# The decode tokens' share of the conformer convolution: taps over the state rows summed once ahead of the group loop

## The chip, the cores and the metric

The kernel runs on one core of one Trainium2 chip. The metric is the device time of one execution in microseconds, as the median of several runs. The core has five engines that run side by side: TensorE (PE; its weight loads are shown as PEld), VectorE (DVE), ScalarE (ACT), GpSimd (POOL) and SyncE (SP), which issues most of the transfers.

## The reference, cut to what matters

One layer of a hybrid decoder is computed for 560 tokens: 8 running sequences with 4 new tokens each (32 "decode" columns), 16 meta tokens and 512 prompt tokens (528 "prompt" columns). One of its two branches is a depthwise causal convolution of 31 taps over 1024 channels:

```python
a = glu_v * jax.nn.sigmoid(glu_g)
a_full = jnp.concatenate([conf_buf, a], axis=1)      # conf_buf: 30 rows of state per running sequence
new_conf_buf = a_full[:, -(CONF_K - 1):]
a = causal_dwconv(a_full, conf_dw_w, conf_dw_b)      # CONF_K = 31 taps, one weight per tap and channel
```

For a decode token r (0 to 3) of a sequence, output r is the sum over the taps j = 0 to 30 of w[j] times row r + j of a_full. Rows 0 to 29 come from the state and rows 30 to 33 are the new tokens. So tap j of token r reads a new token only where r + j is 30 or more, which is in 10 of the 4 x 31 products. The prompt starts from zeros. The other branch is a state-space mixer (convolution of 4 taps, chunked scan, gated norm). After both come output products, and a mixture of 32 experts.

## The kernel before, in words

The kernel has a first stage (`trunk`), an output stage (`mixer`) and the routing and experts. The change is in `trunk` alone. It holds the channels on the 128 partitions and the tokens along the columns.

**Prologue.** State, scales and tokens are loaded, turned by TensorE into the channel layout (`fill`), and copied out of the PSUM banks pS and pT by VectorE (lines 902 to 928). The 30 state rows of the 8 sequences land in `stC`, 240 columns for each of 8 blocks of channels. Then TensorE multiplies the step sizes (line 698, into pC), VectorE waits for that (`s_dtp`), and a short chain over VectorE, ScalarE and TensorE ends in `s_pro`.

**Group loop.** It has eight trips, g = 0 to 7, each over 128 channels of the conformer branch and one of eight groups of the other. TensorE multiplies ten weight blocks a trip (`block`, line 731, each 8 x 3 weight loads with two products of 304 and 256 columns behind each). Every block needs its weights loaded (SP), rounded (ScalarE, line 504) and the rest taken (line 230: POOL for blocks 0 to 5, VectorE for blocks 6 to 9). Blocks 6 to 9 are cut in halves, and between the halves stand the six chunks of the scan: TensorE `stage1(j)` (lines 748 to 757), ScalarE `chunk(j)` (lines 588 to 597), POOL `xtl`, `hTd` and the decay rows of the next chunk (lines 444, 451, 434), VectorE `stage1(j)` (lines 1012 to 1016, which ends with tile Lx), TensorE `stage2(j)` (from line 771, which reads Lx), VectorE `stage2(j)` (to line 1042). The order is written out by hand on each engine, and each engine works in its own order and waits at semaphores.

**The 31 taps.** VectorE spreads them over the trip (`conf_tap`, `taps`): two before its `stage1(0)`, two in front of each of `stage2(0)` to `stage2(4)`, eight before `stage2(5)`, four after the new states, seven at the very end. Each tap is two instructions: a small one of 32 columns from `a_s` (30 state rows and 4 new ones for each sequence) and a big one of 528 columns from `a_p`. All go through the helper on line 871, but for tap 0 on lines 969 and 970. The big one is linked: `k.link` makes VectorE wait until it has ended, so the next tap's small one starts behind it. The small one has no wait behind it. Tap 30 writes `aout`, after a wait for the store of the last group's `aout` (`s_ast`), and SP stores it on line 310 when `s_cconv` comes.

**POOL** copies, at the start of a trip, the group's scales (line 410), the state rows of the other convolution (line 414) and those of this one from `stC` to `a_s` (line 418). VectorE's first work of a trip (line 992) waits for line 414's.

Of the kernel before, what the change touches and what calls it, by code (L numbers as in the profile page):

```python
# [48 lines left out]
DVE_STEPS = 59  # L49
# [42 lines left out]
def trunk(nc, A, O, keep):  # L92
# [5 lines left out]
    with ExitStack() as ctx:  # L98
        def sb(name, shape, dt=F32):
# [25 lines left out]
        stC = sb("stC", [P, KD, NSAMP * (CK - 1)])  # L125
# [21 lines left out]
        a_s = sb("a_s", [P, NSAMP, CK - 1 + TSAMP])  # L147
# [54 lines left out]
        s_ident, s_ss, s_expA, s_stc, s_sts, s_g, s_gst = map(  # L202
            sem, ("s_ident", "s_ss", "s_expA", "s_stc", "s_sts", "s_g", "s_gst"))
# [146 lines left out]
        def _(pool):  # L350
# [50 lines left out]
            def group(g, is_last=False):  # L401
# [36 lines left out]
                for j in range(6):  # L438
# [21 lines left out]
                    if j == 0:  # L460
# [5 lines left out]
                        for q in range(4):  # L466
# [6 lines left out]
                                         a_s[:, :, CK - 1:CK - 1 + TSAMP]).then_inc(s_pk, 1)  # L473
# [12 lines left out]
        def _(act):  # L486
# [34 lines left out]
            act.wait_ge(s_const, 4)  # L521
# [345 lines left out]
        def _(dve):  # L867
# [82 lines left out]
            with dve.Fori(0, G) as g:  # L950
# [7 lines left out]
                def conf_tap(j):  # L958

                    wj = gc[:, R_CW + j:R_CW + j + 1]  # L960
                    outs = (aout if j == CK - 1 else cacc)
                    o_s = outs[:, 0:SAMP].rearrange("p (b r) -> p b r", b=NSAMP)
                    o_p = outs[:, SAMP:T]
                    i_s, i_p = a_s[:, :, j:j + TSAMP], a_p[:, j:j + PROMPT]
                    if j == CK - 1:
                        dve.wait_ge(s_ast, 16 * g + 1)
# [1190 lines left out]
```

## Time and profile before

| what | value |
|---|---|
| median of 3 runs | 1772.03 us |
| the runs | 1772.03, 1772.23, 1767.18 us |
| span of the profiled execution | 1770.0 us |
| PE busy | 1465.9 us (83%) |
| DVE busy | 1348.9 us (76%), 2060 instructions |
| ACT busy | 727.2 us (41%) |
| POOL busy | 395.0 us (22%) |
| mean granted TensorE clock | 0.903 |

The span runs from the first to the last instruction of the profiled execution. That execution's own time is not listed apart from its span; the three timed runs lie between 2.8 us below and 2.2 us above the span. Times within the trace are counted from the start of the span. The group loop fills it from about 82 us to 991 us.

### The profile page before, as it was taken

What the parts mean: (1) busy time and instruction counts of PE and PEld (TensorE: products, weight loads), DVE (VectorE), ACT (ScalarE), POOL (GpSimd) and SP (SyncE); (2) the same over time, 40 slices, a digit from 0 to 9 for tenths busy, and PEclk for the clock granted to TensorE, in tenths of its full rate; (3) what the DMA queues carried; (4) which work ended last, traced back from release to release, by engine and by line L of the source; (5) the groups of instructions that cost most, each with busy time, mean ns of one, the idle gap of its engine ahead of it and who ended that gap; (6) DMA issues with size and microseconds to landing.
All of it is one profiled execution on the core that took longest, in us unless ns stands there. A gap on an engine that the chain in (4) does not pass through costs nothing. (4 is left out here: it accounts for less than half of the span.)

```text
span 1770.0 us, 27567 instructions
## 1 busy us (share of the span) xinstructions
PE 1465.9 (83%) x8979; PEld 1283.1 (72%) x8979; DVE 1348.9 (76%) x2060; ACT 727.2 (41%) x1012; POOL 395.0 (22%) x467
## 2 busy tenths in 40 slices
PE   3898988989889899898998499998338888888880
PEld 2896887968879688796887389986336777676760
DVE  4169888888888888888888636442738999999984
ACT  3132232322323223232232322332028888888871
POOL 1035243352433424334252000000130000000002
PEclk9599897998989989899799699999669999999995
DMA  4031241411414115141160644320359999999966
GB/s 135 24 96 32 79 107 49 130 44 50 135 47 121 54 45 140 40 128 54 42 179 13 202 143 151 120 78 12 105 210 370 369 372 370 370 371 373 369 241 226
DMA packets 187558, 274.00 MB, mean 155 GB/s; under 512 B 11196, under 2 KB 149670, under 8 KB 172118
## 3 DMA queue, kind: packets, MB, share of 16 engines
q1 hardware_dynamic: 174638, 231.85, 40.0%
q10 hardware_dynamic: 8672, 27.86, 4.0%
q0 software_dynamic: 4208, 13.78, 2.2%
q8 instruction: 23, 0.38, 0.1%
q14 instruction: 17, 0.14, 0.0%
HBM read 224.19 MB, written 50.12 MB: 155 GB/s over the span
## 5 line engine op out<-in xcount | busy, mean ns | idle before, releaser
L731 PE MATMUL pu<-xh,wh 128*128 128x304 f32 (+1 forms) x1280 | 289.2, 309 | 5.8 <-ACT zc L651 4.6
L731 PE MATMUL pu<-xl,wh 128*128 128x304 f32 (+1 forms) x1280 | 279.8, 301 | 0.0
L731 PE MATMUL pu<-xh,wl 128*128 128x304 f32 (+1 forms) x1280 | 278.1, 300 | 0.0
L731 PEld LDWEIGHTS pu<-xh,wh 128*128 128x128 f32 x1280 | 206.9, 199 | 10.2 <-issue 9.9
L731 PEld LDWEIGHTS pu<-xl,wh 128*128 128x128 f32 x1280 | 208.7, 199 | 0.0
L731 PEld LDWEIGHTS pu<-xh,wl 128*128 128x128 f32 x1280 | 206.0, 198 | 0.0
L1965 DVE TENSOR_TENSOR W13l<-W,W13h 128x1024 fp32r<-128x1024 f32 x160 | 185.2, 1221 | 11.3 <-ACT W13h L1913 10.7
L230 POOL TENSOR_TENSOR wl<-ring,wh 128x1024 fp32r<-128x1024 f32 x48 | 118.8, 2475 | 330.2 <-ACT wh L504 330.2
L871 DVE SCALAR_TENSOR_TENSOR cacc<-a_p,gc,cacc 128x528 f32<-128x528 f32 x232 | 187.4, 808 | 0.0
L504 ACT ACTIVATE wh<-ring 128x1024 fp32r<-128x1024 f32 x80 | 84.5, 1057 | 218.4 <-PE pu L731 218.3
L1872 PE MATMUL eh<-W13h,xch 128*128 128x512 f32 x320 | 130.6, 408 | 50.5 <-DVE xcl L1965 46.2
L1913 ACT ACTIVATE W13h<-W 128x1024 fp32r<-128x1024 f32 x160 | 156.2, 1051 | 6.2 <-DMA W<-in_exp_w 5.2
L1872 PE MATMUL eh<-W13h,xcl 128*128 128x512 f32 x320 | 126.0, 394 | 0.0
L1872 PE MATMUL eh<-W13l,xch 128*128 128x512 f32 x320 | 126.0, 394 | 0.0
L1872 PEld LDWEIGHTS eh<-W13h,xch 128*128 128x128 f32 x320 | 60.9, 190 | 69.8 <-issue 55.5
L1250 PE MATMUL pm<-yh,vh 128*128 128x304 f32 (+1 forms) x384 | 83.1, 298 | 28.9 <-DVE yl L1362 27.9
L2051 POOL DMA_INDIRECT ye<-slot_rows,pos x10 | 10.4, 1036 | 429.1 <-PEq L2017 426.4
L588 ACT ACTIVATE Lx<-pS 128x512 f32<-128x512 f32 (+2 forms) x48 | 23.1, 480 | 186.5 <-PE pT L757 186.5
L1965 DVE TENSOR_TENSOR W2l<-W,W2h 128x1024 fp32r<-128x1024 f32 x80 | 94.2, 1220 | 1.4 <-PE ey L1890 1.4
L871 DVE SCALAR_TENSOR_TENSOR cv<-raw_p,gc,cv 128x528 f32<-128x528 f32 x96 | 93.7, 976 | 0.0
L444 POOL TENSOR_TENSOR xtl<-Tt,tail 128x256 f32<-128x256 f32 (+2 forms) x48 | 29.3, 611 | 251.2 <-ACT Tt L597 165.6
L1014 DVE TENSOR_TENSOR xdt<-Tt,dtt 128x256 f32<-128x256 f32 (+2 forms) x48 | 77.0, 1603 | 6.9 <-DVE cbm L1012 0.2
(381 smaller groups left out, 3195.9 us busy)
## 6 DMA issues: line engine op xcount, KB each, us to landing
W<-in_exp_w SPq DMA_DIRECT2D x120, 1024.0 KB, 8.2
ring<-in_w_in SPq DMA_DIRECT2D x80, 512.0 KB, 3.9
slot_rows<-yo ACTq DMA_DIRECT2D x40, 512.0 KB, 8.6
x<-in_state_ssm SPq DMA_DIRECT2D x16, 512.0 KB, 7.0
out_new_ssm_sample<-x SPq DMA_DIRECT2D x16, 512.0 KB, 5.3
wraw<-in_ssm_out_w SPq DMA_DIRECT2D x8, 1024.0 KB, 8.2
gates<-gbuf ACTq DMA_DIRECT2D x16, 280.0 KB, 2.1
ssd_rows<-yout SPq DMA_DIRECT2D x8, 560.0 KB, 2.9
```

The source lines that it names most:

```text
L230: return eng.tensor_tensor(wl[:, k % RING], ring[:, k % RING], wh[:, k % RING].bitcast(F32), ALU.subtract)
L444: pool.tensor_tensor(xtl[0:S, :, :], Tt[0:S, 0:2, :].rearrange("s i (h p) -> s (i h) p", h=2), t4, ALU.mult).then_inc(s_xtl, 1)
L504: act.activation(wh[:, k % RING].rearrange("p k m -> p (k m)"), ring[:, k % RING].rearrange("p k m -> p (k m)"), ACT.Copy).then_inc(s_wh, 1)
L588: act.activation(Lx[0:S, :, 0:S], pS[0:S, :].rearrange("s (h t) -> s h t", h=HG)[:, :, 0:S], ACT.Exp).then_inc(s_L, 1)
L731: last = pe.matmul(u_cols(r, a, b), w[:, k % RING, j, :], x[:, j, a:b], start=(j == 0 and n == 0), stop=(j == KD - 1 and n == 2))
L871: return dve.scalar_tensor_tensor(out=out, in0=in0, scalar=scalar, in1=in1, op0=op0, op1=op1)
L1014: dve.tensor_tensor(xdt[0:S, :, :], Tt[0:S, 0:2, :].rearrange("s i (h p) -> s (i h) p", h=2), dt4, ALU.mult)
L1250: last = pe.matmul(cols(pm[r % 2], a, b), w[:, m % 2, w_cols(j)], x[:, j, a:b], start=(j == 0 and n == 0), stop=(j == K - 1 and n == 2))
L1872: last = pe.matmul(ph[b][:, :], x[:, b, j, :], w[:, b, j, :], start=(j == 0 and n == 0), stop=(j == KD - 1 and n == 2))
L1913: act.activation(W13h[:, b, KC * c:KC * c + KC, :].rearrange("p k (a f) -> p a k f", a=2), w13_part(b, c), ACT.Copy).then_inc(s_wh, 1)
L1965: return dve.tensor_tensor(out, whole, high.bitcast(F32), ALU.subtract)
L2051: pool.indirect_dma_start(out=ye[0:S, n, :], out_offset=None, in_=keep["ysc"], in_offset=bass.IndirectOffsetOnAxis(ap=pos[0:S, n:n + 1], a ...
```

## The change

The small instruction of every tap goes. Ahead of the loop, for each of the 8 channel blocks, VectorE multiplies overlapping windows of `stC` (8 sequences x 4 tokens x 30 rows, 960 columns; each sequence now has 33 columns in `stC`, the last three zero) with the 30 weights, and sums the 30 products with a reduce into `cst` (32 columns); one instruction then adds the bias for all blocks. In the loop a new step `conf_new`, ahead of the first taps, adds the products with the new tokens: four linked small instructions of 32, 24, 16 and 8 columns into `aout`. `a_s` holds the 4 new rows alone, so POOL's copy on line 418 and VectorE's wait for it go. POOL clears three columns of `stC` (one memset, ahead of its first split). The wait for `s_ast` moves from tap 30 to `conf_new`.

```diff
-        a_s = sb("a_s", [P, NSAMP, CK - 1 + TSAMP])
+        a_s = sb("a_s", [P, NSAMP, TSAMP])
-        stC = sb("stC", [P, KD, NSAMP * (CK - 1)])
+        stC = sb("stC", [P, KD, NSAMP, CK - 1 + TSAMP - 1])
+        cst = sb("cst", [P, KD, NSAMP, TSAMP])
...
+            pool.memset(stC[:, :, :, CK - 1:], 0.0).then_inc(s_const, 1)
...
-                pool.tensor_copy(a_s[:, :, 0:CK - 1],
-                                 stC[:, g, :].rearrange("p (b r) -> p b r", b=NSAMP)).then_inc(s_stc, 1)
...
-            dve.wait_ge(s_const, 4)
+            dve.wait_ge(s_const, 5)
+            dve.wait_ge(s_fillfree, 17)
+            taps0 = NSAMP * TSAMP * (CK - 1)
+            spare = [zc[:, :, :].rearrange("p i t -> p (i t)"), Ed[:, :, :].rearrange("p i t -> p (i t)")]
+            for m in range(KD):
+                row = NSAMP * (CK - 1 + TSAMP - 1)
+                windows = bass.AP(stC, row * m, [[row * KD, P], [CK - 1 + TSAMP - 1, NSAMP], [1, TSAMP], [1, CK - 1]])
+                w4 = cs[:, m, R_CW:R_CW + CK - 1].unsqueeze(1).unsqueeze(1).broadcast_to([P, NSAMP, TSAMP, CK - 1])
+                prod = spare[m % 2][:, 0:taps0].rearrange("p (b r j) -> p b r j", b=NSAMP, r=TSAMP)
+                k.link(dve.tensor_tensor(prod, windows, w4, ALU.mult))
+                dve.tensor_reduce(cst[:, m, :, :], prod, AX_X, ALU.add).then_inc(s_cst, 1)
+            dve.wait_ge(s_cst, KD)
+            k.link(dve.tensor_tensor(cst[:, :, :, :].rearrange("p m b r -> p m (b r)"),
+                                     cst[:, :, :, :].rearrange("p m b r -> p m (b r)"),
+                                     cs[:, :, R_CB].unsqueeze(2).broadcast_to([P, KD, SAMP]), ALU.add))
             dve.wait_ge(s_dtb, 32)
             dve.wait_ge(s_dtp, 1)
...
                 def conf_tap(j):
                     wj = gc[:, R_CW + j:R_CW + j + 1]
+                    o_p = (aout if j == CK - 1 else cacc)[:, SAMP:T]
+                    i_p = a_p[:, j:j + PROMPT]
                     if j == 0:
-                        bias = gc[:, R_CB:R_CB + 1]
-                        dve.tensor_scalar(o_s, i_s, wj, bias, ALU.mult, ALU.add)
-                        k.link(dve.tensor_scalar(o_p, i_p, wj, bias, ALU.mult, ALU.add))
+                        k.link(dve.tensor_scalar(o_p, i_p, wj, gc[:, R_CB:R_CB + 1], ALU.mult, ALU.add))
                     else:
-                        stt(o_s, i_s, wj, cacc[:, 0:SAMP].rearrange("p (b r) -> p b r", b=NSAMP))
                         ins = stt(o_p, i_p, wj, cacc[:, SAMP:T])
...
+                def conf_new():
+                    o_s = aout[:, 0:SAMP].rearrange("p (b r) -> p b r", b=NSAMP)
+                    dve.wait_ge(s_ast, 16 * g + 1)
+                    for d in range(TSAMP):
+                        wj = gc[:, R_CW + CK - 1 - d:R_CW + CK - d]
+                        k.link(stt(o_s[:, :, d:], a_s[:, :, 0:TSAMP - d], wj,
+                                   cst[:, g, :, :] if d == 0 else o_s[:, :, d:]))
...
-                dve.wait_ge(s_stc, g + 1)
...
+                conf_new()
                 taps(2)
                 stage1(0)
```

## Rows read from the trace of the kernel before

**Rows 1.** Busy time by trip: PE, PEld, DVE, ACT, POOL, PEclk, DMA share, GB/s.

```profile
327.29:439.86 112.57, 101.81 (x694) 90.68 (x693) 99.08 (x171) 34.73 (x58) 43.48 (x50) 0.91 0.29 80
...
552.39:661.87 109.48, 98.72 (x694) 88.67 (x693) 99.09 (x170) 34.73 (x58) 43.53 (x50) 0.94 0.29 82
```

**Rows 2.** Waits from 325 to 437.5 us: total, times, longest.

```profile
POOL wl L230 <- ACT wh L504: 37.8, 5, 16.7
...
PE pY L771 <- DVE Lx L1016: 6.6, 5, 2.3
...
DVE cv L992 <- POOL raw_s L414: 2.9, 1, 2.9
...
DVE cbm L1012 <- ACT Tt L597: 2.5, 2, 2.3
```

**Rows 3.** Timeline of PE, one trip: start, duration, instruction, idle before it.

```profile
368.62 0.50 PE L748 MATMUL pS<-aUh,SLr 128*128 128x512 f32 x1 [1.14 <-POOL aUl L434]
...
375.27 0.66 PE L771 MATMUL pY<-Lx,xdt 128*64 128x128 f32 x8 [2.26 <-DVE Lx L1016]
...
382.44 0.66 PE L771 MATMUL pY<-Lx,xdt 128*64 128x128 f32 x8 [1.32 <-DVE Lx L1016]
...
390.17 0.66 PE L771 MATMUL pY<-Lx,xdt 128*64 128x128 f32 x8 [1.89 <-DVE Lx L1016]
```

**Rows 4.** Timeline of DVE: taps in that trip.

```profile
352.83 0.30 DVE L969 TENSOR_SCALAR cacc<-a_s,gc 128x32 f32<-128x32 f32 x1
...
367.59 1.02 DVE L871 SCALAR_TENSOR_TENSOR cacc<-a_s,gc,cacc 128x32 f32<-128x32 f32 x1
368.54 0.76 DVE L871 SCALAR_TENSOR_TENSOR cacc<-a_p,gc,cacc 128x528 f32<-128x528 f32 x1
369.33 0.25 DVE L871 SCALAR_TENSOR_TENSOR cacc<-a_s,gc,cacc 128x32 f32<-128x32 f32 x1
369.50 0.76 DVE L871 SCALAR_TENSOR_TENSOR cacc<-a_p,gc,cacc 128x528 f32<-128x528 f32 x1
...
432.14 2.90 DVE L871 SCALAR_TENSOR_TENSOR cacc<-a_p,gc,cacc 128x528 f32<-128x528 f32 x1
```

**Rows 5.** Timeline of POOL, same trip.

```profile
366.55 2.02 POOL L434 TENSOR_TENSOR aUl<-aal,U 128x512 fp32r<-128x512 f32 x1
...
432.05 2.43 POOL L230 TENSOR_TENSOR wl<-ring,wh 128x1024 fp32r<-128x1024 f32 x1 [16.73 <-ACT wh L504]
```

**Rows 6.** Timeline of DVE, end of its wait in the prologue.

```profile
72.20 0.67 DVE L935 TENSOR_TENSOR dtt<-pC,dtb 32x32 f32<-32x32 f32 x6 [22.06 <-PE pC L698]
```

**Rows 7.** Groups of instructions: wide product and reduces on DVE, busy us and mean ns.

```profile
L1965 DVE TENSOR_TENSOR W13l<-W,W13h 128x1024 fp32r<-128x1024 f32 x160 | 185.2, 1221 | 11.3 <-ACT W13h L1913 10.7
L1600 DVE TENSOR_REDUCE exf<-cmp 1x40 f32<-1x1280 f32 x2 | 2.9, 1474 | 0.1
L1600 DVE TENSOR_REDUCE posf<-part 128x10 f32<-128x320 f32 x1 | 0.5, 486 | 0.0
```

**Rows 8.** Tile a_s: POOL's copy (min/median/max ns, first and last start).

```profile
L418 POOL COPY a_s<-stC x8: 379/385/389, 101.6 to 887.1; 128x240 f32 x7, 128x240 f32<-128x240 f32 x1
```

**Rows 9.** Store of aout: issue on SP's timeline, and time to landing.

```profile
337.39 0.36 SPq L310 DMA_DIRECT2D conv_rows<-aout  x1
...
DMA to landing us min/median/max: 2.1/3.5/3.5
```

**Rows 10.** Timeline where the loop ends: last tap, its store, first mixer work.

```profile
990.38 0.76 DVE L871 SCALAR_TENSOR_TENSOR aout<-a_p,gc,cacc 128x528 f32<-128x528 f32 x1
991.17 0.36 SPq L310 DMA_DIRECT2D conv_rows<-aout  x1
...
994.83 1.91 ACT L1295 ACTIVATE vh<-wraw 128x2048 fp32r<-128x2048 f32 x1 [15.66 <-PEq L89]
```

**Rows 11.** Busy time by stretch, same columns as rows 1.

```profile
391.00:398.00 7.00, 6.55 (x30) 5.16 (x30) 6.17 (x10) 1.92 (x5) 3.28 (x3) 0.52 0.10 41
398.00:405.00 7.00, 6.61 (x61) 6.33 (x60) 6.86 (x11) 1.09 (x2) 1.52 (x1) 0.99 0.28 75
```

More of the change, by code:

```diff
@@ L48 @@
 POOL_LOW = 6
-DVE_STEPS = 59
+DVE_STEPS = 63
 N_CROW = 18
@@ L201, in trunk @@
         s_pk, s_out, s_outev = map(sem, ("s_pk", "s_out", "s_outev"))
-        s_ident, s_ss, s_expA, s_stc, s_sts, s_g, s_gst = map(
-            sem, ("s_ident", "s_ss", "s_expA", "s_stc", "s_sts", "s_g", "s_gst"))
+        s_ident, s_ss, s_expA, s_cst, s_sts, s_g, s_gst = map(
+            sem, ("s_ident", "s_ss", "s_expA", "s_cst", "s_sts", "s_g", "s_gst"))
         s_ds0, s_dsr, s_settled = sem("s_ds0"), sem("s_dsr"), sem("s_settled")
@@ L472, in group @@
                         pool.tensor_copy(pa[:, CK - 1:62].rearrange("p (r b) -> p b r", b=NSAMP),
-                                         a_s[:, :, CK - 1:CK - 1 + TSAMP]).then_inc(s_pk, 1)
+                                         a_s[:, :, :]).then_inc(s_pk, 1)
                 if not is_last:
@@ L520, in _ @@
             act.activation(tmp2[:, :, :], tmp2[:, :, :], ACT.Ln, bias=1.0).then_inc(s_dtl, 1)
-            act.wait_ge(s_const, 4)
+            act.wait_ge(s_const, 5)
             act.activation(SLr[:, :], SL[:, :], ACT.Copy).then_inc(s_slr, 1)
@@ L919, in _ @@
                     dve.wait_ge(s_fill, n + 1)
-                    dve.tensor_copy(stC[:, 4 * h:4 * h + 4, 120 * t:120 * t + 120],
-                                    (pS, pT)[n % 2][:, :].rearrange("p (q s) -> p q s", q=4)[:, :, 0:120])\
-                       .then_inc(s_fillfree, 1)
+                    rows = (pS, pT)[n % 2][:, :].rearrange("p (q s) -> p q s", q=4)[:, :, 0:120]
+                    dve.tensor_copy(stC[:, 4 * h:4 * h + 4, 4 * t:4 * t + 4, 0:CK - 1],
+                                    rows.rearrange("p q (b r) -> p q b r", b=4)).then_inc(s_fillfree, 1)
                     n += 1
@@ L960, in conf_tap @@
                     wj = gc[:, R_CW + j:R_CW + j + 1]
[L961 to L966, printed above, removed]
+                    o_p = (aout if j == CK - 1 else cacc)[:, SAMP:T]
+                    i_p = a_p[:, j:j + PROMPT]
                     if j == 0:
-                        bias = gc[:, R_CB:R_CB + 1]
-                        dve.tensor_scalar(o_s, i_s, wj, bias, ALU.mult, ALU.add)
-                        k.link(dve.tensor_scalar(o_p, i_p, wj, bias, ALU.mult, ALU.add))
+                        k.link(dve.tensor_scalar(o_p, i_p, wj, gc[:, R_CB:R_CB + 1], ALU.mult, ALU.add))
                     else:
-                        stt(o_s, i_s, wj, cacc[:, 0:SAMP].rearrange("p (b r) -> p b r", b=NSAMP))
                         ins = stt(o_p, i_p, wj, cacc[:, SAMP:T])
@@ L1053, in _ @@
                 dve.wait_ge(s_ufree, U_TILES * g + 6 + 1)
-                dve.wait_ge(s_stc, g + 1)
                 dve.wait_ge(s_pk, 7 * g + 1)
                 dve.wait_ge(s_cconv, g + 1)
-                stt(a_s[:, :, CK - 1:], zc[:, 1, 0:SAMP].rearrange("p (b r) -> p b r", b=NSAMP), 1.0,
+                stt(a_s[:, :, :], zc[:, 1, 0:SAMP].rearrange("p (b r) -> p b r", b=NSAMP), 1.0,
                     zc[:, 0, 0:SAMP].rearrange("p (b r) -> p b r", b=NSAMP), ALU.add, ALU.mult).then_inc(s_ga, 1)
```

## The prediction

> **What bounds the kernel now.** I read the busy time by trip first [rows 1]. A trip of the group loop takes 112.5 us, of which TensorE is busy 101.8 and VectorE 99.1. Both are nearly full, so the question is who waits for whom. The list of waits of one trip [rows 2] answers it: TensorE waits 6.6 us for VectorE's Lx, in five pieces. The other way round VectorE waits 2.5 us for ScalarE's Tt in front of its stage1(0), and 2.9 us for POOL at the start of a trip. So TensorE sets the trip, and VectorE matters where its Lx ends TensorE's wait. The timeline of TensorE [rows 3] places these: 2.26, 1.32 and 1.89 us ahead of stage2(2), stage2(3) and stage2(4), 5.5 of the 6.6 us. From the Lx of stage1(1) to that of stage1(4), which releases TensorE at 390.17, VectorE never idles: it works through the rest of block 8, two taps, stage2(1), stage1(2), two taps, stage2(2), stage1(3), the rest of block 9, two taps, stage2(3), stage1(4). This stretch is VectorE's own chain, and six taps lie in it.
>
> **What a small instruction costs.** On the timeline of VectorE [rows 4] the small one lasts 0.25 us, but the big one behind it starts 0.17 us after it (369.33 and 369.50), because nothing makes it wait. The small one itself starts 0.03 us after the big one before it has ended (368.54 + 0.76, then 369.33). So a tap now takes 0.96 us, and without the small one the next big one takes its place after the same link: 0.79. I take **0.17 us** for each. The bounds: 0.29 if the whole small one and a link went (0.25 + 0.04), zero where something else holds the engine. Such a place is the first tap after the rest of a block: its small one starts at 367.59 and lasts 1.02 us, and ends as POOL's aUl does (366.55 + 2.02 = 368.57, against 367.59 + 1.02 = 368.61) [rows 4, 5]. It stands still while POOL works. Does the big one, put there, lose as much? The nearest row is the big tap at 432.14, which began just after POOL's 2.43 us piece at 432.05 and ended at 435.04, 0.56 us after that piece. The pair at 367.59 ended at 369.30, 0.73 after POOL. The difference is again 0.17. I take it there too, with zero as the other bound.
>
> **The sum in the loop.** Removed: 31 small ones a trip, 31 x 0.17 = 5.3 us of VectorE. Added by conf_new: four linked small ones, 4 x (0.25 + 0.04) = 1.2 us. On TensorE's path lie only the six taps of the chain: 6 x 0.17 = 1.02 us a trip, as 0.34, 0.68 and 1.02 us off the three waits of rows 3, which are longer than that each time, so VectorE still ends them. I take 1.0 us a trip, 8.0 for eight; bounds 3 x 0.17 = 0.5 a trip (nothing at the taps behind POOL) and 6 x 0.29 = 1.7. The other taps are off the path. The taps before stage2(0) and those in front of stage2(4) lead to VectorE waiting for Tt or pC. The eight before stage2(5), the four after the states and the seven at the trip's end run beside TensorE's products; what they free turns into VectorE waiting, and the 2.9 us for POOL [rows 2] grows, because POOL's raw_s stands behind its rest of block 3, which waits for ScalarE and TensorE.
>
> **conf_new** sits between stage1(0)'s wait and the work before it. It adds 1.2 and the two taps there give back 0.34, so 0.8 us more; the 2.5 us wait for Tt in rows 2 (2.3 the longest piece) hides it. Without that cover it would cost 0.8 us a trip, 6.5 in all, since Lx of stage1(0) is waited for. The wait for the aout store moves to conf_new: what is queued behind it is all of VectorE's stage work, and TensorE behind that. In the trip read the store is issued by SP at 337.39 and lands 3.5 us later at most [rows 9], at 340.9, while conf_new would start where tap 0 does now, at 352.83 [rows 4]: 11.9 us to spare. SP's order is unchanged.
>
> **POOL** loses one copy of 0.385 us a trip [rows 8]. It stands ahead of a rest that waits for ScalarE's wh anyway (37.8 us a trip for five such waits [rows 2]): nothing. The memset added is short and runs while POOL waits in the prologue. VectorE's dropped wait on that copy never ended last.
>
> **The prologue.** VectorE gets 8 products of 960 columns, 8 reduces from 960 to 32 and one add of 256. It stands idle 22.06 us there, until TensorE's small products end [rows 6]. A product of 1024 columns takes 1.221 us, so 960 take 1.15. Reduces from 320 and 1280 columns take 0.486 and 1.474 us [rows 7]; on the line between them 960 take 1.15. With a link's 0.04 each, 8 x 2.38 = 19.0, and at most 0.5 for the last: 19.5 us, **hidden with 2.5 us to spare**. By the wider rows (1.221 and 1.474) it would be 8 x 2.78 + 0.5 = 22.7, exposed by 0.7. Counted as nothing; bounds 0 and +0.7. The row of the wide product reads plain tiles, and half of the windows here start at an odd word. [...] No row here shows such a read.
>
> **The end of the loop.** After the last group's norm the seven last taps run alone: tap 30 ends at 991.14, its store is issued at 991.17, and the mixer's first instruction starts at 994.83 [rows 10]. Here all seven small ones are on the path: 7 x 0.17 = 1.2 us.
>
> **Sum:** 8.0 + 1.2 + 0 = 9.2 us less. The profiled span of 1770.0 us becomes 1760.8. The median of the runs is 2.0 above that span, so I forecast **1772.0 - 9.2 = 1762.8 us**. A difference of 0.3%, 5.3 us, is about what a measurement of this kernel can tell from none.
>
> **The rivals.**
>
> *The clock gives more.* In the trip from 327.29, which stands for the five others like it, TensorE's granted clock averages 0.91; in the trip from 552.39 it is 0.94, and that trip is 3.1 us shorter (109.48 against 112.57) with the same work [rows 1]. Within a trip the clock falls to 0.52, that is to 1.2 GHz, at about 391 us, after the stretch of VectorE-bound waits, and is back at 2.4 GHz at 398 [rows 11]. Shorter waits could make more trips of the 0.94 kind: each gives 3.1 us, two more give 9.2 + 6.2 = 15.4 us, 1756.6. For it: the gain falls just ahead of the fall of the clock. Against: 4.5 us of waits stay, and one trip of eight is all the trace shows. The Trainium skill (TensorE: Matmul & The Clock Gate, "What's actually happening") says that the array is throttled by default and activity releases it, which points this way; the direction agrees with rows 11, the amount isn't told.
>
> *The gain is swallowed.* TensorE also waits for POOL's aUl (1.14 us [rows 3]), and POOL's pieces hold VectorE [rows 4, 5]. If these take the place of the small ones, and half a chain's gain remains, it is 0.5 x 8 + 1.2 = 5.3 us or less; with the clock's stretches covering the work that now comes earlier, half of that again: 1767 to 1770. For it: the small tap held for 1.02 us shows that POOL can stop this chain. Against: POOL's pieces there follow VectorE's hT and Tt and shift along.
>
> *The change doesn't do what it says:* the small one is worth less than 0.17 because a big tap directly behind a big one starts later than a small one does. The 0.03 us behind a link speaks against. It would give the same figure as the last.
>
> *Slower: the clock takes back.* The stretch from 398 to 405 us is at 0.99 now [rows 11]. If TensorE's earlier arrival puts its thin work (the products of four columns) so that this stretch stays at 1.2 GHz, its 6.6 busy us take up to twice as long for half of it, +3.3 us a trip. Against the gain of 9.2 it decides from three trips (+9.9, 1772.7); in five it gives +16.5 - 9.2, 1779.3. For it: the kernel of before has one such shift the other way. Against: no trip of the trace shows a longer form.
>
> **Chances.** Forecast 0.50, the clock gives more 0.17, swallowed (with "doesn't do what it says") 0.25, slower 0.08. Of the forecast's own case 0.06 falls short of 5.3 us. So faster by over 0.3% 0.61, within 0.3% 0.31, slower 0.08. The range runs from 1756, two more trips with the short form, to 1771, which takes in most of the swallowed case and leaves out the slower one and three trips or more of the short form.
>
> **What would show it.** In the profile after: taps 0.79 to 0.80 us apart; VectorE busy some 30 us less in the loop; PE waits for Lx down from 6.6 to about 5.6 us a trip; trips at 111.5 us; the wait for pC in the prologue down from 22.06 to about 2.5 us and still there; 1.2 us less from the last yout to the mixer. Wrong would be: that wait gone and the first trip late; the Lx wait unchanged or a new one on the store in conf_new; trips still at 112.5 us with taps at 0.8 (the clock or POOL took it); trips of several lengths (the clock decides).

## The result, and the profile after

| what | before | after |
|---|---|---|
| median | 1772.13 us (4 runs, 1767.18 to 1773.7) | **1740.93 us** (4 runs, 1738.85 to 1744.7) |
| ratio, 95% interval | | 0.983 [0.981, 0.9851] |
| span of the profiled execution | 1770.0 us | 1742.9 us (its own time 1744.7) |
| mean granted TensorE clock | 0.903 | 0.915 |

The gain is 31 us where 9.2 was forecast, and 1740.9 lies below the range. A run more than 1.5% above the fastest of its kernel is left out of medians and ratios below; only one of e17 was, with 1754.1 us. The page of after, its span and busy times:

```profile
span 1742.9 us, 27387 instructions
PE 1446.2 (83%) x8979; PEld 1271.1 (73%) x8979; DVE 1330.8 (76%) x1861; ACT 725.5 (42%) x1012; POOL 397.0 (23%) x460
```

**Where the time went.** The busy time by stretch, first of before: the six trips from 214.74 and the mixer and experts behind the loop (columns as in [rows 1]).

```profile
214.74:886.93 672.19, 607.66 (x4149) 541.96 (x4148) 594.37 (x1020) 207.08 (x347) 261.18 (x290) 0.91 0.29 80
994.88:1770.00 775.12, 608.35 (x3173) 516.74 (x3173) 536.22 (x647) 428.51 (x507) 42.06 (x59) 0.92 0.69 251
```

Then of after: the same six trips, two of them alone, and the rest behind the loop.

```profile
209.65:856.10 646.45, 587.24 (x4149) 526.10 (x4148) 567.02 (x858) 206.09 (x347) 264.18 (x284) 0.95 0.30 83
316.86:426.35 109.49, 99.13 (x694) 88.61 (x693) 95.15 (x143) 34.56 (x58) 43.79 (x49) 0.94 0.29 82
535.42:640.98 105.56, 96.05 (x694) 86.20 (x693) 94.05 (x143) 34.56 (x58) 44.12 (x49) 0.97 0.30 85
960.23:1742.90 782.67, 615.88 (x3173) 525.45 (x3173) 536.21 (x647) 428.10 (x507) 41.90 (x59) 0.91 0.68 249
```

Two things are to be seen. The six trips are 25.7 us shorter with the same 4149 products of TensorE, and their granted clock rises from 0.91 to 0.95. Time by clock, 0.91 x 672.19 = 611.7 and 0.95 x 646.45 = 614.1, is the same within the rounding of the clock: TensorE's work and waits, counted at full clock, changed by little. And the stage behind the loop, which the change doesn't touch, took 7.6 us longer in this execution, at 0.91 against 0.92. So several us either way come without any change of the work, and the loop's part of the gain is read from the loop.

The trace also records the granted clock as such. For the six trips it has 116.1 us at 1.2 GHz before and 64.9 us after. Half of the difference is 25.6 us. I use this below as bookkeeping for every kernel: **low** is that time, and **the rest** is the six trips' time less half of low, about what they would take at 2.4 GHz throughout. It is not exact, since TensorE isn't busy in all of a low stretch: single trips of e1 give rests from 102.2 to 104.0 us, so a difference of 2 or 3 us in the sum of six means nothing. Half is also on the high side. In before the trip of 109.48 us has 6.8 us less low than the others and is 3.1 us shorter, 0.45 us for one of low; at that price the clock gives 23 of the 25.7 us, and 2.6 are left for shorter waits.

Where in a trip? The stretches of 7 us from 43 us after the start of the trip on in before (trip from 327.29), and from 64 us on in after (from 316.86):

```profile
370.29:377.29 7.00, 4.74 (x38) 4.18 (x37) 6.66 (x12) 2.85 (x5) 3.85 (x4) 1.00 0.13 38
377.29:384.29 7.00, 5.68 (x46) 5.16 (x45) 6.67 (x11) 1.09 (x2) 3.85 (x4) 1.00 0.00 0
384.29:391.29 7.00, 5.11 (x43) 4.62 (x42) 6.59 (x16) 2.77 (x4) 2.57 (x4) 1.00 0.28 82
391.29:398.29 7.00, 6.55 (x30) 5.16 (x29) 6.21 (x9) 1.92 (x5) 3.57 (x3) 0.51 0.09 34
```

```profile
380.86:387.86 7.00, 5.89 (x47) 5.25 (x47) 6.76 (x8) 2.86 (x7) 4.79 (x3) 1.00 0.07 28
387.86:394.86 7.00, 6.83 (x49) 6.79 (x50) 6.73 (x9) 0.03 (x1) 0.00 (x0) 0.73 0.28 75
```

Before, the clock falls 64 us into the trip, behind the three waits of [rows 3], while TensorE is busy 6.55 of 7 us with 30 products. After, the same place runs at 1.00. This **stretch at 64 us** is there in all six trips of before and in none of after; what is left are falls from about 72 to 74 and 84 to 86 us on.

**The waits** in the six trips, 210 to 860 us of before, and then of after (total, times, longest):

```profile
PE pY L771 <- DVE Lx L1016: 39.7, 30, 2.3
PE pS L748 <- POOL aUl L434: 6.9, 6, 1.1
PE pu L819 <- ACT zc L577: 6.3, 6, 1.1
```

```profile
PE pY L769 <- DVE Lx L1030: 31.7, 36, 2.0
PE pS L746 <- POOL aUl L432: 13.7, 12, 1.1
PE pu L817 <- ACT zc L575: 4.4, 6, 0.8
```

Together 52.9 and 49.8 us: 0.5 us a trip, not 1.0. The timeline of TensorE after, the trip that answers to [rows 3]:

```profile
357.90 0.50 PE L746 MATMUL pS<-aUh,SLr 128*128 128x512 f32 x1 [1.14 <-POOL aUl L432]
...
364.28 0.66 PE L769 MATMUL pY<-Lx,xdt 128*64 128x128 f32 x8 [2.01 <-DVE Lx L1030]
...
370.50 0.66 PE L769 MATMUL pY<-Lx,xdt 128*64 128x128 f32 x8 [0.40 <-DVE Lx L1030]
...
373.38 0.50 PE L746 MATMUL pS<-aUh,SLr 128*128 128x512 f32 x1 [1.14 <-POOL aUl L432]
...
379.12 0.66 PE L769 MATMUL pY<-Lx,xdt 128*64 128x128 f32 x8 [1.38 <-DVE Lx L1030]
...
596.77 0.66 PE L769 MATMUL pY<-Lx,xdt 128*64 128x128 f32 x8 [0.93 <-DVE Lx L1030]
```

The three waits fell by 0.25, 0.92 and 0.51 us, but the wait for POOL's aUl now comes twice: the Lx that came earlier let TensorE reach it before POOL had it ready.

This is the after trip that gained least. The product behind the Lx of stage1(4) shows how far TensorE is ahead of any fall of the clock. In before it starts 62.9 us into each of the six trips (390.17 - 327.29). In after it starts 61.36, 62.26, 61.82, 61.35, 61.78 and 61.77 us into them (379.12 - 316.86 is the second, 596.77 - 535.42 the fourth), 1.15 us earlier in the mean. No trip of the twelve has its clock below 1.00 up to there. So 6.9 of the 25.7 us were gained ahead of the falls, and 18.9 behind them, where TensorE has the same products. How much of the 6.9 lasts to the end of a trip can't be told from the clock's part; the clock's part is between these 19 and the 25.6 of the bookkeeping.

Where do the 1.15 us come from? Start to start, VectorE's chain from the Lx of stage1(1) to that of stage1(4) took 24.64 us in each trip before, and after 23.43 to 24.32, in the mean 23.80: 0.84 less, where the forecast has 1.02. (The other 0.3 is POOL's copy, see e9.) Two of the three pairs of taps in it save 0.33 each, 2.67 to 2.34 us, in all six trips. The third, which ran alone before, now starts beside POOL's aUl and lasts longer, in all six trips too. VectorE before, then POOL and VectorE after:

```profile
384.29 0.24 DVE L871 SCALAR_TENSOR_TENSOR cacc<-a_s,gc,cacc 128x32 f32<-128x32 f32 x1
...
385.41 0.76 DVE L871 SCALAR_TENSOR_TENSOR cacc<-a_p,gc,cacc 128x528 f32<-128x528 f32 x1
```

```profile
371.31 2.02 POOL L432 TENSOR_TENSOR aUl<-aal,U 128x512 fp32r<-128x512 f32 x1
...
372.35 2.34 DVE L869 SCALAR_TENSOR_TENSOR cacc<-a_p,gc,cacc 128x528 f32<-128x528 f32 x2
```

The pair with its small ones took 1.88 us, the pair without them 2.34. VectorE doesn't idle in this stretch in either kernel.

### The profile page after: what moved, and what is told of

Read it like the earlier page. It is cut to its first block and busy times, and to the rows that moved or that the text cites. A ratio compares the mean times of both kernels' runs of the same rounds, so it can differ in the third digit from the quotient of the medians.

```text
span 1742.9 us, 27387 instructions
## 1 busy us (share of the span) xinstructions
PE 1446.2 (83%) x8979; PEld 1271.1 (73%) x8979; DVE 1330.8 (76%) x1861; ACT 725.5 (42%) x1012; POOL 397.0 (23%) x460
## 5 line engine op out<-in xcount | busy, mean ns | idle before, releaser
L729 PE MATMUL pu<-xh,wh 128*128 128x304 f32 (+1 forms) x1280 | 283.9, 304 | 6.5 <-ACT zc L649 5.4
L729 PE MATMUL pu<-xl,wh 128*128 128x304 f32 (+1 forms) x1280 | 274.9, 297 | 0.0
L729 PE MATMUL pu<-xh,wl 128*128 128x304 f32 (+1 forms) x1280 | 274.0, 296 | 0.0
L869 DVE SCALAR_TENSOR_TENSOR cacc<-a_p,gc,cacc 128x528 f32<-128x528 f32 x232 | 211.9, 914 | 6.2
L729 PEld LDWEIGHTS pu<-xh,wh 128*128 128x128 f32 x1280 | 202.5, 195 | 10.4 <-issue 10.1
L729 PEld LDWEIGHTS pu<-xl,wh 128*128 128x128 f32 x1280 | 204.0, 195 | 0.0
L729 PEld LDWEIGHTS pu<-xh,wl 128*128 128x128 f32 x1280 | 201.9, 194 | 0.0
L442 POOL TENSOR_TENSOR xtl<-Tt,tail 128x256 f32<-128x256 f32 (+2 forms) x48 | 31.7, 661 | 240.4 <-ACT Tt L595 158.0
L1264 PE MATMUL pm<-yl,vh 128*128 128x304 f32 (+1 forms) x384 | 81.3, 293 | 0.0
```

Source lines behind the costliest of these rows:

```text
L442: pool.tensor_tensor(xtl[0:S, :, :], Tt[0:S, 0:2, :].rearrange("s i (h p) -> s (i h) p", h=2), t4, ALU.mult).then_inc(s_xtl, 1)
L729: last = pe.matmul(u_cols(r, a, b), w[:, k % RING, j, :], x[:, j, a:b], start=(j == 0 and n == 0), stop=(j == KD - 1 and n == 2))
L869: return dve.scalar_tensor_tensor(out=out, in0=in0, scalar=scalar, in1=in1, op0=op0, op1=op1)
L1264: last = pe.matmul(cols(pm[r % 2], a, b), w[:, m % 2, w_cols(j)], x[:, j, a:b], start=(j == 0 and n == 0), stop=(j == K - 1 and n == 2))
```

## The experiments

All runs, each against the kernel before on the same chip, whose median was 1774.98 us in the batch of e1 to e4, 1769.07 (e5 to e8), 1767.35 (e9 to e12), 1771.32 (e13 to e15) and 1774.01 (e16, e17). T, low and rest are those of six trips of the profiled execution; Lx, aUl and zc are TensorE's waits there for VectorE's Lx, POOL's aUl and ScalarE's zc ahead of the decay-row products (us); n is the number of trips, of six, with the stretch at 64 us. The column "profiled" has the time of the profiled execution, which isn't always near the median: e4, e14 and e17 were profiled in one of their fastest executions, e6 and e10 in their slowest.

| run | median | minus before | ratio [95%] | profiled | T | low | rest | Lx | aUl | zc | n |
|---|---|---|---|---|---|---|---|---|---|---|---|
| before (profile above) | 1772.1 |  |  | 1770.0 (span) | 672.2 | 116.1 | 614.2 | 39.7 | 6.9 | 6.3 | 6 |
| after | 1740.9 | -31.2 | 0.983 [0.981, 0.9851] | 1744.7 | 646.5 | 64.9 | 614.0 | 31.7 | 13.7 | 4.4 | 0 |
| e1_all31 | 1765.8 | -9.2 | 0.9953 [0.9929, 0.9977] | 1766.3 | 662.1 | 88.7 | 617.7 | 38.8 | 8.9 | 6.4 | 4 |
| e2_chain6 | 1758.4 | -16.6 | 0.9904 [0.9867, 0.994] | 1759.7 | 662.7 | 95.6 | 614.9 | 42.1 | 6.9 | 4.3 | 3 |
| e3_rest25 | 1751.9 | -23.1 | 0.987 [0.9824, 0.9916] | 1753.4 | 658.1 | 75.1 | 620.5 | 35.4 | 13.7 | 4.7 | 0 |
| e4_before_filled | 1760.8 | -14.2 | 0.9928 [0.9904, 0.9951] | 1753.9 | 662.1 | 75.1 | 624.5 | 13.6 | 5.6 | 7.8 | 0 |
| e5_before_moved | 1777.2 | +8.1 | 1.0053 [1.0031, 1.0075] | 1777.6 | 679.1 | 119.5 | 619.4 | 18.5 | 14.7 | 15.1 | 0 |
| e6_after_moved | 1739.6 | -29.5 | 0.984 [0.9788, 0.9892] | 1755.0 | 655.3 | 68.3 | 621.2 | 16.8 | 14.7 | 7.6 | 0 |
| e7_before_shifted | 1774.4 | +5.4 | 1.0019 [0.999, 1.0048] | 1775.4 | 673.0 | 116.1 | 614.9 | 39.2 | 7.7 | 6.8 | 5 |
| e8_after_filled | 1735.2 | -33.9 | 0.9841 [0.9776, 0.9905] | 1731.0 | 643.5 | 58.0 | 614.5 | 9.2 | 12.5 | 4.3 | 0 |
| e9_before_nocopy | 1759.6 | -7.8 | 0.9957 [0.9932, 0.9983] | 1759.7 | 658.6 | 81.9 | 617.7 | 39.3 | 7.9 | 5.5 | 5 |
| e10_after_thinfilled | 1750.4 | -16.9 | 0.9888 [0.9839, 0.9936] | 1756.5 | 656.1 | 78.5 | 616.9 | 30.7 | 12.6 | 4.5 | 0 |
| e11_before_new | 1772.3 | +5.0 | 1.0014 [0.999, 1.0038] | 1772.2 | 672.1 | 116.1 | 614.1 | 39.6 | 6.9 | 6.5 | 6 |
| e12_after_again | 1738.5 | -28.9 | 0.9832 [0.9789, 0.9875] | 1738.1 | 648.6 | 68.3 | 614.5 | 32.0 | 12.6 | 4.5 | 0 |
| e13_before_three | 1772.3 | +1.0 | 1.0002 [0.9974, 1.003] | 1773.7 | 672.8 | 109.2 | 618.2 | 19.3 | 14.7 | 15.1 | 0 |
| e14_after_three | 1731.4 | -40.0 | 0.9778 [0.9719, 0.9836] | 1727.3 | 638.8 | 61.4 | 608.1 | 16.7 | 17.5 | 7.2 | 0 |
| e15_after_six | 1752.1 | -19.3 | 0.9883 [0.9828, 0.9938] | 1751.3 | 655.7 | 81.9 | 614.8 | 16.6 | 14.7 | 15.1 | 0 |
| e16_after_side | 1743.3 | -30.7 | 0.9824 [0.9797, 0.9852] | 1742.8 | 655.3 | 81.9 | 614.3 | 32.6 | 13.7 | 4.5 | 0 |
| e17_three_side | 1733.9 | -40.1 | 0.9786 [0.974, 0.9833] | 1723.9 | 639.4 | 61.4 | 608.7 | 16.8 | 17.5 | 7.7 | 0 |

### Which part gives the gain

The small instructions come back into after as idle ones: as large, in the same place, with a result that nobody reads. e1 has all 31, e2 those of the six taps of the chain alone, e3 the other 25. e4 is the kernel before with unread products of TensorE in the waits ahead of stage2(2), (3) and (4): the same waits, but not idle.

```diff
# after.py, conf_tap: e1 range(CK), e2 range(4, 10), e3 (0 to 3, 10 to 30)
+                    if j in range(4, 10):
+                        stt(idle[:, :].rearrange("p (b r) -> p b r", b=NSAMP), a_s[:, :, :], wj, cst[:, g, :, :])
# before.py, TensorE's stage2(j): e4
+                    pe.wait_ge(s_y, 6 * g + j + 1)
+                    pe.wait_ge(s_outev, 3 * g + 1)
+                    for _ in range({2: 16, 3: 9, 4: 14}.get(j, 0)):
+                        pe.matmul(pY[:, 256:512], SLr[:, :], xh[:, 0, 0:256], start=True, stop=True)
                     pe.wait_ge(s_W, 6 * g + j + 2)
                     pe.wait_ge(s_xtl, 6 * g + j + 2)
-                    pe.wait_ge(s_y, 6 * g + j + 1)
-                    pe.wait_ge(s_outev, 3 * g + 1)
```

> The changed kernel with a small instruction of 32 columns, into a tile that nobody reads, put back ahead of all 31 big taps. It keeps the new prologue, conf_new and the shorter work of POOL. Theory 1 (the small instructions are what mattered, by way of the waits ahead of the clock's fall): back near the kernel before, 1765 to 1776 us, trips of about 112.5 us with three stretches at the lower clock in each. Rival (POOL's lost copy, the prologue or the new order of the waits did it): it stays near 1741 us plus at most the 6 us of the small ones on the path.

> The changed kernel with the small instruction put back at taps 4 to 9 alone, the six between the Lx of stage1(1) and that of stage1(4). Theory 1 (these six decide whether the clock falls right behind the waits for Lx): most of the gain goes, 1760 to 1775 us. Rival (the clock depends on the whole trip's length or on work elsewhere in it): 1741 to 1750 us, the six cost no more than their 1 us a trip.

> The mirror of the run with six: small instructions at the 25 taps outside the chain, none at taps 4 to 9. Theory 1: the gain stays but for the seven at the end of the last trip, 1741 to 1746 us. Rival (the work off TensorE's path matters by way of the trip's phase): 1755 to 1775 us.

> The kernel before, with products of 256 columns that nobody reads issued by TensorE while it waits for Lx ahead of stage2(2), stage2(3) and stage2(4): 16, 9 and 14 of them, about as long as the waits of 2.26, 1.32 and 1.89 us. No real work is removed, so VectorE's chain is as long as before. Theory 1 (the gain is the clock's, which falls after those waits): much of the gain comes without the change, 1740 to 1755 us, and the stretch at the lower clock that began at 391.4 us is gone from the trip. Rival (the gain is the time of VectorE's instructions): 1771 us or slower by what the products overrun.

The differences within this batch: with all small ones back 9.2 us of the gain are left (e1). Taking the six of the chain out is worth 1765.8 - 1751.9 = 13.9 us (e3 against e1); taking the other 25 out 1765.8 - 1758.4 = 7.4 us (e2 against e1). 9.2 + 13.9 + 7.4 = 30.5, about the whole gain: the parts add up. e1 came in at the low end of its theory's range, but e2 and e3 lie between the range of the theory and that of the rival, and e4 gained less than its theory had. Per tap the six are worth 13.9 / 8 / 6 = 0.29 us a trip, the others, less 1.2 us at the loop's end, 6.2 / 8 / 25 = 0.03.

e4 removes no work, and gains 14.2 us. Its six trips from 209.96:

```profile
209.96:872.01 662.05, 619.72 (x4383) 561.44 (x4382) 595.34 (x1020) 205.92 (x347) 257.45 (x290) 0.94 0.29 82
...
361.99:368.99 7.00, 6.60 (x56) 6.09 (x54) 6.63 (x12) 3.20 (x5) 3.66 (x4) 1.00 0.28 75
368.99:375.99 7.00, 6.75 (x56) 6.30 (x54) 6.63 (x13) 1.09 (x2) 3.68 (x5) 1.00 0.00 0
375.99:382.99 7.00, 7.00 (x55) 6.53 (x51) 6.63 (x13) 2.60 (x4) 2.49 (x5) 1.00 0.26 75
382.99:389.99 7.00, 6.51 (x53) 5.41 (x53) 6.77 (x11) 1.97 (x6) 3.62 (x4) 1.00 0.10 41
```

TensorE is busy 6.60 to 7.00 us of each 7 where before it was 4.74 to 5.68, and the stretch at 64 us is gone in all six trips. The 234 extra products cost 8 to 10 us and low falls by 41.0, which gives back 18 to 20 (at 0.45 or 0.5 us for one of low); together the six trips are 10.1 us shorter. What brings the clock down at 64 us is thus TensorE's idle time in these waits, not the small instructions as such. But the outcome can't be read off one stretch. Two trips of e2, stretches from 57 and from 64 us on:

```profile
382.36:389.36 7.00, 5.12 (x43) 4.72 (x41) 6.59 (x13) 2.76 (x4) 2.56 (x4) 0.97 0.33 100
389.36:396.36 7.00, 6.55 (x31) 5.15 (x31) 5.82 (x8) 1.92 (x5) 3.84 (x3) 0.54 0.04 16
...
603.64:610.64 7.00, 5.13 (x43) 4.56 (x41) 6.59 (x13) 2.76 (x4) 2.56 (x4) 1.00 0.35 102
610.64:617.64 7.00, 6.11 (x49) 5.31 (x47) 6.59 (x8) 2.65 (x7) 4.80 (x3) 1.00 0.04 14
```

The same work, 5.12 and 5.13 us busy, and the clock falls behind the one and not behind the other. Over all profiled trips with the six small ones in place, the taps where they were and the waits not filled (before, e1, e2, e7, e9, e11), the fall comes in 29 of 36; without the small ones (after, e12, e16, e3) or with the waits filled (e4, e8) in none of 36. The count isn't the whole price. In four of the seven trips without it (two of e1, one each of e7 and e9) two shorter falls come at 23 and 50 us instead, and e1 has the fall in four trips but shorter ones behind it, and so less low than before.

### The 9.2 us that are not the small instructions

e9 is the kernel before without POOL's copy into `a_s` (it leaves the state's share of the decode tokens out); e11 is before with four linked small ones where conf_new stands, unread.

```diff
# e9, before.py
+            pool.memset(a_s[:, :, 0:CK - 1], 0.0).then_inc(s_stc, 1)
...
-                pool.tensor_copy(a_s[:, :, 0:CK - 1],
-                                 stC[:, g, :].rearrange("p (b r) -> p b r", b=NSAMP)).then_inc(s_stc, 1)
...
-                dve.wait_ge(s_stc, g + 1)
+                dve.wait_ge(s_stc, 1)
# e11, before.py, ahead of the first taps(2)
+                for d in range(TSAMP):
+                    k.link(stt(idle[:, :, d:], a_s[:, :, 0:TSAMP - d],
+                               gc[:, R_CW + CK - 1 - d:R_CW + CK - d], a_s[:, :, 4:4 + TSAMP - d]))
```

> The kernel before without POOL's copy of the state rows in each trip (line 418) and without VectorE's wait on it; the state rows are cleared once ahead of the loop, so the state's share of the decode tokens' convolution is left out. All 62 instructions of the taps stay. Theory 1, after the run with 31 small ones put back came out 9 us under the kernel before: POOL's shorter start of a trip (its split of block 4 and the products' rows come 0.4 us earlier) or conf_new's new pace is worth some of that; here 1760 to 1768 us if it is POOL's copy. Rival: the copy is hidden, 1769 to 1777 us, as the kernel before on the same chip.

> The kernel before with four linked small instructions like those of conf_new, into a tile that nobody reads, added ahead of tap 0; nothing else is changed. They lie in VectorE's wait for Tt ahead of stage1(0). Theory 1: hidden, 1769 to 1777 us. Rival (they push Lx of stage1(0) or, by moving VectorE's taps against POOL, take part in the 9 us): off the kernel before by more than 5 us either way.

The copy alone is worth 7.8 us, most of e1's 9.2. conf_new costs nothing that can be told: +5.0 us with an interval of the ratio from 0.999 to 1.0038, and the six trips are 672.1 against 672.2. How does a copy of 0.385 us on a nearly idle engine [rows 8] reach the end? The timelines of a trip's start (VectorE and POOL) and of TensorE's wait ahead of the decay-row products, before and then e9:

```profile
327.29 0.53 DVE L992 TENSOR_SCALAR cv<-raw_s,gc 128x32 f32<-128x32 f32 x1 [2.87 <-POOL raw_s L414]
327.40 0.39 POOL L418 COPY a_s<-stC 128x240 f32 x1
327.74 0.54 DVE L993 TENSOR_SCALAR cv<-raw_p,gc 128x528 f32<-128x528 f32 x1
330.58 2.87 POOL L230 TENSOR_TENSOR wl<-ring,wh 128x1024 fp32r<-128x1024 f32 x1 [2.79 <-ACT wh L504]
350.46 0.40 PE L819 MATMUL pu<-Ub,ab 32*128 32x32 f32 x2 [1.05 <-ACT zc L577]
```

```profile
324.69 0.30 DVE L990 TENSOR_SCALAR cv<-raw_s,gc 128x32 f32<-128x32 f32 x1 [2.87 <-POOL raw_s L415]
324.90 0.55 DVE L991 TENSOR_SCALAR cv<-raw_p,gc 128x528 f32<-128x528 f32 x1
327.98 2.64 POOL L230 TENSOR_TENSOR wl<-ring,wh 128x1024 fp32r<-128x1024 f32 x1 [3.12 <-ACT wh L502]
...
347.57 0.40 PE L817 MATMUL pu<-Ub,ab 32*128 32x32 f32 x2 [0.76 <-ACT zc L575]
```

Not through POOL's next piece, which starts 3.29 us into the trip in both (330.58 and 327.98). It is VectorE that gains: its first convolution instruction stands beside POOL's copy and lasts 0.53 to 0.55 us in the eight trips of before, 0.30 to 0.36 in those of e9. In the trips shown the second one starts 0.21 instead of 0.45 us into the trip. VectorE works through from there to its last convolution, which is 0.3 us earlier, and with it come ScalarE's zc and TensorE's products, 22.88 us into the trip instead of 23.17. It is 0.3 us in each of eight trips, 2.4 us; the rest is low, 81.9 us against 116.1. The stretch at 64 us stays in five of six trips, but the later falls are shorter. Why 0.3 us there shortens them isn't shown.

### Is it the place in time? Is it the thin products?

e7 delays the loop of before by 3 us in the prologue (two unread operations of 1120 columns on VectorE). e8 fills the waits of after, with 14, 3 and 9 products. e10 sets the same product seven times between the 32 products of four columns in after's stage2(5). e12 is after again.

```diff
# e7, before.py, behind the sum into dtt
+            k.link(dve.memset(zc[:, :, :], 0.0))
+            k.link(dve.tensor_tensor(zc[:, :, :], zc[:, :, :], zc[:, :, :], ALU.add))
# e10, after.py, behind each product of four columns
+                                if b % 2 == 1 and (i, b) != (1, 7):
+                                    pe.matmul(pY[:, 256:512], SLr[:, :], xh[:, 0, 0:256], start=True, stop=True)
```

> The kernel before with two instructions of VectorE, a memset and a sum over 1120 columns, some 2 us in all, put into the prologue's chain ahead of the loop, so that all trips come 2 us later against the clock's own time base and nothing in the loop is changed. Theory 1 (the work of a trip brings the clock down): about 1773 to 1779 us, the kernel before plus 2 us, three stretches a trip. Rival (the kernel before only happened to lie badly in time, and any shift breaks the pattern of three stretches): 1745 to 1766 us.

> The changed kernel with products that nobody reads in the waits ahead of stage2(2), stage2(3) and stage2(4): 14, 3 and 9. Theory 1: no stretch at the lower clock began right behind these waits in the changed kernel, so filling them brings nothing more: 1738 to 1750 us. Rival (the waits still cost clock in the stretches that are left): 1720 to 1735 us.

> The changed kernel with seven products of 256 columns, which nobody reads, between the 32 products of four columns of stage2(5). Theory: the stretch at the lower clock that starts some 74 us into each trip follows on that thin work; with it filled, the stretch is shorter or gone, and the trip loses up to 3.4 us against some 0.9 us that the fill costs: 1720 to 1738 us. Rival (the stretch comes from elsewhere): 7 us slower than the changed kernel on the same chip.

> The changed kernel itself, on the same chip as the others of this call: 1736 to 1746 us. If parts add, this is the kernel before less 9 (all small ones put back), less 14 (the six in the chain), less 7 (the other 25), that is some 31 us less.

e7: the loop starts at 104.43 instead of 101.46, and low, trips and the stretch at 64 us stay (116.1 us, 5 of 6). The median moves by 5.4 us, with an interval that holds both 0 and the delay of 3. This shift of the whole loop doesn't change the clock, which speaks against the gain of after being an accident of where the trips begin. Other shifts weren't tried. e8: the products fit into the waits (rest 614.5, Lx waits 9.2) and low is 58.0; the six trips are 3 us shorter than after's, and the median of 1735.2 is the lowest of its batch, but its interval reaches from 0.9776 to 0.9905 and holds that of after. e10 missed: with the thin products no longer alone, the fall from 74 us on is still there in all six trips, low is 78.5 (64.9 to 81.9 in the three profiles of after), and the median is 12 us above e12's. What starts the fall at 74 us stays open.

### Taps moved

Can the same be had by moving taps out of the chain, with nothing removed? The taps ahead of stage1(0), behind it and in front of stage2(1) to (4) go from 2, 2, 2, 2, 2, 2 to 4, 2, 0, 0, 0, 2 (six moved; on the chain none is left) or 3, 2, 1, 1, 1, 2 (three moved).

```diff
# before.py or after.py; shown: e5, e6. Taps by slot: e5, e6: 4,2,0,0,0,2 / 10 / 4 / 9;  e15: 4,2,0,0,0,2 / 8 / 4 / 11;  e13, e14, e17: 3,2,1,1,1,2 / 8 / 4 / 9
-                taps(2)
+                taps(4)
                 stage1(0)
...
-                        taps(2)
+                        taps((0, 0, 0, 0, 2)[j])
-                taps(8)
+                taps(10)
-                taps(7)
+                taps(9)
```

> The kernel before with its 31 taps and their small instructions all kept, but the six taps between the Lx of stage1(1) and that of stage1(4) moved: two to the slot ahead of stage1(0), two more before stage2(5), two more at the end of the trip. Theory 1 (waits for Lx bring the clock down behind them, and the waits are VectorE's chain): the chain loses 5.8 us, so TensorE's 5.5 us of waits mostly go, 2 to 4 us a trip, and the stretch at the lower clock some 64 us into the trip goes with them, 3.4 us more a trip; 1.9 us more at the end of the loop: 1720 to 1750 us. Rival (only fewer instructions on VectorE help): 1765 us or more.

> The kernel before with all its instructions, and three of the six taps of the chain moved into idle time of VectorE: one ahead of stage1(0), where it waits 2.3 us for Tt, and two at the end of the trip, where it waits 2.9 us for POOL. The chain is 2.9 us shorter, and nothing new is waited for. Theory (the waits for Lx start the stretch 64 us into the trip): that stretch is gone, 2 to 3 us less of waits in each trip, 1.9 us more at the end of the loop: 1735 to 1755 us. Rival (it takes fewer instructions on VectorE): 1765 to 1775 us.

On before this gains nothing: e5 is 8.1 us slower, e13 is within 1.0 us. Both theories missed. The waits of e13 say why (210 to 860 us):

```profile
PE pY L771 <- DVE Lx L1016: 19.3, 36, 1.2
PE pu L819 <- ACT zc L577: 15.1, 6, 2.5
PE pS L748 <- POOL aUl L434: 14.7, 18, 1.1
PE pS L809 <- DVE x L871: 5.4, 6, 1.8
```

The Lx waits fall from 39.7 to 19.3, and the zc waits rise from 6.3 to 15.1, aUl from 6.9 to 14.7 and those for VectorE's x from 2.2 to 5.4. The sum is 54.5 against 55.1, and another wait for zc (line 573), 2.2 us, is new. The stretch at 64 us is gone, but the clock falls from 72 to 75 us on, for longer than in after, and low is 109.2. VectorE, busy 594 of 672 us, is a second full engine: a tap moved off the chain is late somewhere else.

> The same move of six taps on the changed kernel. Theory 1: the waits for Lx that are left there (2.0, 0.4 and 1.4 us in the trip read) go too, 2 to 3 us a trip for eight trips, less 1.6 us for two more taps at the end of the loop: 1715 to 1735 us. Rival (the change already took what the clock gives, and POOL's aUl or the thin work sets the rest): 1738 to 1745 us.

> The changed kernel with all six taps out of the chain: two more ahead of stage1(0), four more at the end of the trip, where the wait for POOL of 4.0 us takes 3.2. Theory: POOL's aUl and ScalarE's Tt then set TensorE's waits, 1 us a trip less than with three moved, and 3.2 us more at the end of the loop: 1718 to 1735 us. Rival (the taps at the end of a trip push the next one's start and ScalarE's zc): 1738 us or more.

> The same move of three taps on the changed kernel. Theory: the waits ahead of stage2(2) and stage2(4), 2.0 and 1.4 us, shrink by 0.8 us a slot, the trip by 1.5 to 2.5 us, 1.6 us more at the end of the loop: 1722 to 1732 us, a kernel faster than both. Rival (the clock's remaining stretches take the place of what is gained): 1736 to 1745 us.

> The changed kernel, beside the one with three taps moved: 1736 to 1744 us.

> The changed kernel with three taps of the chain moved, on the same chip. Theory (its shorter waits for Lx are worth some 1.5 us a trip, and the clock follows in some trips): 5 to 12 us under the changed kernel beside it. Rival (chip and chance): within 4 us of it.

On after, six moved is no gain (e6, 1739.6) or a loss (e15, 1752.1), as the rivals had it. TensorE's wait for VectorE's x is 21.1 us in e6's six trips, its zc wait 15.1 in e15's. But e15's six trips take no longer than e16's (655.7 and 655.3): of the 8.5 us between the two profiled executions 7.2 lie between the start of the last trip and the mixer, where four more taps stand (3.2 us). With three moved, the six trips of two executions on two chips are 638.8 and 639.4 us, with rests of 608.1 and 608.7: here 6 us of real waiting are gone, 1 us a trip. The medians were 1731.4 in one batch, and side by side 1733.9 (five runs) against 1743.3 for after, with runs from 1723.4 to 1745.7 and from 1739.0 to 1748.6. The version may beat after; the runs overlap and don't settle it.

## Why the prediction was wrong

- **"VectorE's small instruction is worth 0.17 us":** right. Eight taps take 6.40 us (timeline below), 0.80 each; forecast 0.79 to 0.80.
- **"6 x 0.17 = 1.02 us a trip":** the place was right, the size nearly. VectorE's chain got 0.84 us shorter in the mean of six trips, and from trip to trip 0.3 to 1.2. "POOL's pieces there shift along" was wrong: the third pair of taps now falls beside POOL's aUl and loses 0.46 us, as the rival "swallowed" had it for a part. All waits of TensorE together gave 0.5 us a trip.
- **"The other taps are off the path":** wrong. The 25 gave 7.4 us, the 1.2 at the end among them; with them back TensorE's waits for Lx are 35.4 instead of 31.7 us (e3 and after).
- **"POOL's copy: nothing":** wrong, 7.8 us. I looked at who waits for POOL's next piece, and not at what VectorE does beside the copy: the instruction there took 0.54 instead of 0.30 us, and 0.3 us a trip reached TensorE. [rows 4, 5] had shown me the same thing at another place.
- **The failed step** is the one that isn't in the sum: that the granted clock stays as it was. "Shorter waits could make more trips of the 0.94 kind" named the mechanism, and it was given 0.17 and priced as two more trips at 3.1 us. In fact the stretch at 64 us, which I had read in [rows 11] as the stretch behind the waits, went in every trip, 41 of the 51 us by which low fell, and the falls behind it got shorter; together they make up between 19 and all of the 25.7 us of six trips. My argument against, one short trip of eight, counted trips of a kernel whose waits were unchanged, and says nothing of what shorter waits do. The trip of 109.48 in [rows 1] still had its fall at 64 us; its later ones were shorter. Read right, one stretch less is worth 3.1 us a trip by the same rows, 25 us in eight trips. That all eight would lose it couldn't be known from the trace of before.
- **conf_new, 0.8 us hidden:** right. It takes 0.24 + 0.78 us, and TensorE has no wait behind it; VectorE's wait for Tt went from 2.5 to 1.6 us. Its wait for the store of `aout` never ended last.
- **The prologue, 19.5 us hidden with 2.5 to spare:** right; the wait for pC is 3.38 us. The product of 960 columns takes 1150 ns and the reduce 1153, both forecast as 1.15 us.
- **The end of the loop, 1.2 us:** right. The seven taps take 950.89 to 956.48, 5.6 us, against 984.42 to 991.14, 6.7.
- **"Slower: the clock takes back":** not seen.

The timeline of VectorE after: the wait for pC in the prologue, conf_new, eight taps, the last taps; then its two new groups of instructions.

```profile
72.25 0.67 DVE L947 TENSOR_TENSOR dtt<-pC,dtb 32x32 f32<-32x32 f32 x6 [3.38 <-PE pC L696]
...
342.11 0.24 DVE L869 SCALAR_TENSOR_TENSOR aout<-a_s,gc,cst 128x32 f32<-128x32 f32 x1
342.38 0.78 DVE L869 SCALAR_TENSOR_TENSOR aout<-a_s,gc,aout 128x24 f32<-128x24 f32 x3
...
389.25 6.40 DVE L869 SCALAR_TENSOR_TENSOR cacc<-a_p,gc,cacc 128x528 f32<-128x528 f32 x8
...
950.89 4.78 DVE L869 SCALAR_TENSOR_TENSOR cacc<-a_p,gc,cacc 128x528 f32<-128x528 f32 x6
955.71 0.77 DVE L869 SCALAR_TENSOR_TENSOR aout<-a_p,gc,cacc 128x528 f32<-128x528 f32 x1
```

```profile
L938 DVE TENSOR_TENSOR zc<-stC,cs 128x960 f32<-128x960 f32 x4 | 4.6, 1150 | 0.1
L939 DVE TENSOR_REDUCE cst<-zc 128x32 f32<-128x960 f32 x4 | 4.6, 1153 | 0.1
```

## What to carry to other kernels

Where TensorE's granted clock dips inside a loop, waits of TensorE ahead of a dip can cost twice: once as waits, once as work at 1.2 GHz behind them. So read the clock by stretches before summing waits, and give a case of its own to "the dip goes", priced as the whole dip in every trip (here some 3 us, read off two trips of before). Where two engines are nearly full, work moved to another place can come back as another wait, as in e5 and e13. And ask of a short operation on a third engine not only who waits for it, but what runs beside it.

## What the runs showed of the hardware

- Unread products in TensorE's waits made a kernel faster, 1760.8 against 1775.0 us, with no work removed (e4). The Trainium skill (TensorE: Matmul & The Clock Gate, "What's actually happening") has the array throttled by default and released by activity. The direction agrees; how much idle time lets the clock fall, these runs don't show, and e2's two trips with the same 5.1 us busy and different clocks speak against reading it off one stretch.
- One kernel differs by several us between executions through the clock: after's six trips took 646.5, 648.6 and 655.3 us with rests of 614.0, 614.5 and 614.3.
- VectorE's instructions last longer beside POOL's: one of 32 columns 0.53 to 0.55 instead of 0.30 to 0.36 us beside a copy (before, e9), a pair of taps 2.34 instead of 1.88 us beside the product into aUl (after, before), although the pair of before has two small instructions more.
- Half of the windows of 30 words that the 960-column product reads start on an odd word. The Trainium skill (Vector Engine (DVE) Microarchitecture Reference, section 5.2) has 1.30 instead of 1.054 ns a column for pairs that start on an odd word in both sources. That isn't quite this case, with long runs and one such source, and no extra cost is seen here: the product takes 1150 ns, 1.20 a column with all that is fixed in it, as on the plain tiles of [rows 7] (1221 for 1024, 1.19).
